# Down product of an expert ahead of the next expert's gate and up products, and early loads of ScalarE's function tables, in a two-layer mixer with 32 experts

## What is computed

```python
hdn = jax.nn.silu(xe @ w_gate[e]) * (xe @ w_up[e])     # 1024 -> 512
y_e = hdn @ w_down[e]                                  # 512 -> 1024
x   = x + gt2 * sum_of_two(gate * y_e)                 # after both layers: final RMSNorm
```

## Time and profile before

| | us |
|---|---|
| median of 3 runs (1959.91 to 1963.07) | 1959.96 |
| the profiled execution, its own time | 1950.96 |
| span of the profiled execution | 1949.1 |
| TensorE busy (matmul) | 1636.3 (84%) |
| VectorE busy | 622.2 (32%) |
| ScalarE busy | 447.4 (23%) |
| GpSimd busy | 209.1 (11%) |
| data moved by DMA | 527.50 MB |

### The profile page before, as it was taken

One profiled execution on the slowest core, in us unless ns is written; L12 is line 12 of the kernel. 1 busy time (PEld: TensorE's weight loads), 2 busy tenths in 40 slices (PEclk: granted clock), 3 DMA queues, 4 the chain that ended last, 5 costly groups with the idle time before them and its releaser, 6 DMA issues. The chain is left out here.

```text
span 1949.1 us, 22716 instructions
## 1 busy us (share of the span) xinstructions
PE 1636.3 (84%) x7580; PEld 809.3 (42%) x7580; DVE 622.2 (32%) x1333; ACT 447.4 (23%) x1003; POOL 209.1 (11%) x215
## 2 busy tenths in 40 slices
PE   4999987898878998888869999879689788888883
PEld 2455544454333333333335555454434333333331
DVE  1256365233222122222153825631421212221214
ACT  2110645311111111111121026551121111111112
POOL 2000022011111011111020002011110101110110
PEclk7999978998989999999979998889799989998987
DMA  9422434137999999999972324420499999999994
GB/s 340 166 87 96 164 112 143 44 138 282 405 403 401 377 400 408 402 415 412 388 255 69 126 75 161 149 87 22 144 364 379 402 413 405 404 411 395 396 398 186
DMA packets 119092, 527.50 MB, mean 271 GB/s; under 512 B 17008, under 2 KB 23248, under 8 KB 69872
## 3 DMA queue, kind: packets, MB, share of 16 engines
q1 hardware_dynamic: 101520, 493.66, 65.1%
q0 software_dynamic: 13104, 24.51, 4.0%
q10 hardware_dynamic: 4400, 8.46, 1.1%
HBM read 521.06 MB, written 23.86 MB: 280 GB/s over the span
## 5 line engine op out<-in xcount | busy, mean ns | idle before, releaser
L1182 PE MATMUL ps<-ring,arena 128*64 128x512 f32 x2928 | 701.2, 638 | 157.5 <-DMA ring<-in_w_exp_up 130.2
L1182 PEld LDWEIGHTS ps<-ring,arena 128*64 128x64 f32 x2928 | 252.1, 146 | 563.0 <-issue 532.4
L889 PE MATMUL ps<-ring,hT 128*128 128x512 f32 (+1 forms) x1024 | 373.6, 523 | 6.6 <-ACT tmp L1358 4.9
L889 PEld LDWEIGHTS ps<-ring,hT 128*128 128x128 f32 x1024 | 196.5, 195 | 166.5 <-issue 148.4
L622 DVE TENSOR_TENSOR arena<-ps,arena 64x512 f32<-64x512 f32 (+1 forms) x64 | 44.4, 693 | 662.7 <-ACT arena L1455 581.2
L1455 ACT ACTIVATE arena<-ps 128x512 f32<-128x512 f32 x64 | 38.2, 598 | 621.8 <-PE ps L1182 576.0
L1447 ACT ACTIVATE arena<-ps,modc 128x128 f32<-128x128 f32 x256 | 96.5, 457 | 264.6 <-PE ps L1167 264.5
L854 POOL DMA_INDIRECT yexp_d<-arena,masks x64 | 59.3, 927 | 902.6 <-DVE arena L632 902.6
L1589 DVE SCALAR_TENSOR_TENSOR probsT<-z,convw,probsT 128x512 f32<-128x512 f32 x120 | 90.0, 751 | 3.9
L630 DVE TENSOR_TENSOR arena<-ps,gate 64x512 f32<-64x512 f32 (+1 forms) x64 | 43.7, 683 | 145.6 <-PE ps L1182 131.1
L611 DVE TENSOR_SCALAR arena<-ps,modc 128x128 f32<-128x128 f32 x256 | 87.5, 405 | 7.0 <-PE ps L1167 3.6
(11 more groups left out here) (198 smaller groups left out, 1285.3 us busy)
## 6 DMA issues: line engine op xcount, KB each, us to landing
ring<-in_w_exp_gate SPq DMA_DIRECT2D x128, 1024.0 KB, 15.7
ring<-in_w_exp_up SPq DMA_DIRECT2D x128, 1024.0 KB, 19.0
ring<-in_w_exp_down SPq DMA_DIRECT2D x128, 1024.0 KB, 12.5
ring<-in_w_ada SPq DMA_DIRECT2D x24, 2048.0 KB, 8.8
ring<-in_w_in SPq DMA_DIRECT2D x8, 2048.0 KB, 20.4
ring<-in_w_out SPq DMA_DIRECT2D x4, 2048.0 KB, 7.8
ring<-in_w_in SPq DMA_DIRECT2D x6, 1024.0 KB, 10.5
xn_d<-arena ACTq DMA_DIRECT2D x8, 512.0 KB, 4.8
```

The lines of the kernel that those rows point to most:

```text
L889: last = pe.matmul(out, lhs(k), rhs(k), start=(k == 0), stop=(k == n - 1))
L1182: last = [pe.matmul(outs[c][HALF * c:HALF * c + HALF, :], lhs(k)[:, 0:HALF], rhs(c, k), start=(k == 0), stop=(k == n - 1), tile_position=( ...
```

## The change

TensorE runs down(e) straight after turn_hidden(e), ahead of gate_up(e+1); VectorE runs expert_rows(e) ahead of expert_hidden(e+1). ScalarE's, GpSimd's and SyncE's orders in the expert stage stay. On ScalarE, three activations of one column into a new tile `spare` are added in each layer: a square root after the issues of the row loads in `combine`, a square root before the loop that follows the attention, and a silu after the router's exponentials.

```diff
@@ tiles @@
+        spare = sb("spare", [P, 1])
@@ experts_dve @@
             expert_tokens(1, 1)
+            expert_rows(0, 0, 0)
             expert_hidden(1, 0, 1)
-            expert_rows(0, 0, 0)
             expert_tokens(2, 0)
+            expert_rows(1, 0, 1)
             expert_hidden(2, 1, 0)
-            expert_rows(1, 0, 1)
             expert_tokens(3, 1)
             with dve.Fori(1, HE - 1) as it:
+                expert_rows(2 * it, it, 0)
                 expert_hidden(2 * it + 1, it, 1)
-                expert_rows(2 * it, it, 0)
                 expert_tokens(2 * it + 2, 0)
+                expert_rows(2 * it + 1, it, 1)
                 expert_hidden(2 * it + 2, it + 1, 0)
-                expert_rows(2 * it + 1, it, 1)
                 expert_tokens(2 * it + 3, 1)
+            expert_rows(NE - 2, HE - 1, 0)
             expert_hidden(NE - 1, HE - 1, 1)
-            expert_rows(NE - 2, HE - 1, 0)
             expert_rows(NE - 1, HE - 1, 1)
@@ tensor @@
                     turn_hidden(2 * it, 0)
+                    down(2 * it, it, 0)
                     gate_up(2 * it + 1, it, 1)
-                    down(2 * it, it, 0)
                     turn_tokens(2 * it + 2, it + 1, 0)
                     turn_hidden(2 * it + 1, 1)
+                    down(2 * it + 1, it, 1)
                     gate_up(2 * it + 2, it + 1, 0)
-                    down(2 * it + 1, it, 1)
                     turn_tokens(2 * it + 3, it + 1, 1)
                 turn_hidden(NE - 2, 0)
+                down(NE - 2, HE - 1, 0)
                 gate_up(NE - 1, HE - 1, 1)
-                down(NE - 2, HE - 1, 0)
                 turn_hidden(NE - 1, 1)
                 down(NE - 1, HE - 1, 1)
@@ scalar, combine, after the row loads are issued @@
+                act.activation(spare[:, :], C["eps"], ACT.Sqrt)
@@ scalar, after the router's exponentials @@
+                act.activation(spare[:, :], C["eps"], ACT.Silu)
```

## The result

The changed kernel has a median of 1933.78 us (4 runs, 1932.45 to 1942.38) beside 1959.93 us before: ratio 0.9883, 95% interval 0.9859 to 0.9908. Two later comparisons with more runs gave 0.9898 (0.9879 to 0.9917) and 0.9895 (0.9872 to 0.9918), so some 20 us of 1957. The forecast of 1945 us had the sign and most of the mechanism. It stands 11 us above this first median, and its gain of 15 us is 5 short of the 20 that the later ratios give. The profiled execution has a span of 1932.5 us against 1949.1.

What follows compares the result with a forecast made beforehand. The prediction took the DMA weight stream, 16.2 us an expert, to bound the expert stages. Starts 7.5, wide experts 3.0 and ends 3.7 give 14.2, rounded to 15 us off the 1959.96 us median: 1945 us, range 1930 to 1956.

Steps and rivals of the forecast that it cites:

- What bounds the stage: Expert stages: the DMA engines' weight stream sets the pace, 16.2 us an expert at 404 GB/s; TensorE has spare time.
- The rule: Expert stages: the end moves only by idle DMA time between loads and TensorE's work after the last up weights land.
- Part 1: TensorE's own cycle per expert in the new order: 13.85 us at full clock, under the stream's 16.2, so no steady gain.
- Part 2: Start of each expert stage: idle DMA time goes because down(0) frees its slot earlier; 7.5 us for both layers.
- Part 3: Behind experts with more than 64 tokens: most idle DMA time goes as loads are released earlier; 3.0 us, bounds 0 and 4.2.
- Part 4: End of each expert stage: down(30) runs before the last landing, so down(31) starts 1.84 us earlier, 3.7 us in all.
- Part 5: ScalarE's function table loads, moved to idle time or earlier: 0 us, upper bound 2.6 us.
- The sum: Whole kernel: starts, wide experts and ends give 14.2 us, taken as 15 with some tenths for small ragged slices.
- TensorE as the bound: Expert stages: pauses around the hidden turn lower TensorE's clock, cycle 17.25 us, kernel slower at 1997 us; chance 8%.
- The third rival: More is won: wide-expert gain whole, tables on the path, stream above 404 GB/s; 1935 us or less; chance 13%.

Runs made afterwards that it cites:

- light pair: Kernel before and changed kernel, each weight load from the third expert on moving a quarter of its bytes: 1814.65 and 1851.20 us.
- light_after: Changed kernel with each weight load from the third expert on moving a quarter of its bytes: 1851.20 us, beside 1814.65 in the old order.
- start_only: Kernel before with the new order for experts 0 and 1 of each stage only: ratio to before 0.9944.
- the middle alone: Kernel before with the new order for experts 2 to 30 only, old order at experts 0, 1 and the last: ratio to before 0.9987.
- end_only: Kernel before with the new order for the last expert of each stage only: ratio to before 1.0002.
- before_again: Kernel before, unchanged, profiled a second time: ratio 0.9992.
- tables_only: Kernel before with only the early function table loads on ScalarE added, order unchanged: ratio to before 0.9998.

## Why the prediction was right, and where it was short

- **What bounds the stage** was right: the light pair shows from the other side that the stream was the cover, since without it the change loses 37 us. The rule that the end moves only through idle DMA time and the end of the stage holds in layer 0, where experts 20 to 30 are spaced at 15.9 and 16.0 us. In layer 1 it left something out: the stream itself ran 1.5% faster, 4 to 5 us.
- **Part 1** was right to 0.1 us: a cycle of 13.85 us, measured 13.8 to 13.9 at the start of the stages and 13.9 in light_after. Two small slips: the pause before the hidden turn was put at 0.5 us, while its own terms, 1.53 less 1.16, give 0.37 (measured 0.45 to 0.55), and the pauses alone can lower the clock now and then, as light_after shows.
- **Part 2**, the starts, predicted 7.5 us: start_only has 9.1 to silu(30), 9.5 to gate_up(31), 10.1 to down(31) and 11 by its ratio. Right in mechanism, a fifth or more too small; the bytes missing in the two holes give 8.6.
- **Part 3** is the step that failed, in its size: predicted 3.0 us, bounds 0 and 4.2. To the start of gate_up(31) the middle alone measures 6.7 us and 14.9 - 9.5 = 5.4 on top of the starts. I read the loss from the busy share, and took 1.2 us off for a lag that did no harm; the bytes moved in the same windows would have given 6.6. The windows behind the wide experts are full now, but no run had the wide experts alone, and in layer 1 the faster stream is in the same sum.
- **Part 4**, the ends, predicted 1.84 us each: in the changed kernel the down product starts 2.2 us earlier after gate_up(31). The premise, that down(30) then lies before the last landing, holds in the changed kernel and not in end_only. The difference of 0.4 is that down(31) no longer waits for VectorE to empty its banks of down(30)'s rows (the pause before it is 0.69 us, where the earlier trace rows have 0.98), and that the turn starts 1.44 us behind the silu instead of my 1.53. What of it reaches the end was only seen in end_only: there 0.9 us of layer 0's 2.2 were left where the next layer's projections run.
- **Part 5**, the tables, predicted 0: ratio 0.9998.
- **The sum.** The terms give 14.2 us; the 0.8 that make it 15 had no row. Starts and wide experts were put at 10.5 us and measure 14.9 (to gate_up(31)); the ends were put at 3.7 and measure 20.0 - 14.9 = 5.1. To the last silu of layer 1 the first profile of before was 2.4 and 3.2 us quicker than before_again and tables_only, and so 16.6 us between the two first profiles agreed with my 15 by chance.
- **The rivals.** TensorE as the bound was wrong for this kernel, and the clock went the other way: the waits for weights are now 61.0 / 36 = 1.7 us instead of 3.0, the mean clock is 0.942 instead of 0.920. The Trainium skill ("TensorE: Matmul & The Clock Gate", section "HAM oscillation") sees the danger in waits for data between short pieces of compute; the trace agrees that the long waits mattered, and the reordering cut them into shorter ones. The third rival came true in part. Its sign, a rate above 404 GB/s, is there: 411 in the window at 1640 us, and 405 instead of 401 over 1700 to 1860 us. Part 3 came whole, and the first median, 1933.78 us, lies in its "1935 or less". The tables gave nothing, and in layer 0 the experts kept their pace.

## What to carry to other kernels

In a stage that streams weights through a ring, use the slots in the order in which they are loaded: a use out of order holds back every load behind it, and most of the price shows where the queue runs dry, at the start and behind slow pieces. Measure such holes by the bytes that are missing, not by the busy share. Read a partial change by the whole stage, to its last product: the middle alone had 8.8 us at expert 30 and 2.6 at the end. A reordering that puts pauses on the compute engine is free only as long as the stream covers them; how much cover there is can be measured by loading a quarter of the bytes.

## What the runs showed of the hardware that was not expected

The DMA share falls slowly at the end of a stream, as if the 16 engines did not finish together. DMA slices of the changed kernel, 1860 to 1900 us, 1 us each:

```profile
DMA  9999999999999999999997654544333441110000
GB/s 451 410 401 426 422 447 369 336 418 434 410 410 442 434 410 410 410 442 406 438 410 295 254 229 205 213 180 180 139 164 131 160 152 74 78 61 16 0 0 16
```

No load of the ring is issued after about 1873 us, and the share falls from 9 tenths at 1881 step by step to 1 tenth at 1895, while gate_up(31) still waits for its weights until 1889.5. Before the change the fall took about 5 us. I read it so: a deeper queue lets the quicker engines run ahead by as much as the ring allows, and a load has landed only when the slowest engine has brought its share. No row of these traces names a single engine, so this is a reading and not shown. What it costs can be seen from the bytes. Queue q1 from the start of the span to 956.84 us before and to 948.72 us after, which is 486.3 and 476.0 us from layer 0's first silu:

```profile
q1 hardware_dynamic: 54169, 251.45, 67.5%
q1 hardware_dynamic: 54210, 251.43, 67.7%
```

The bytes are 10.3 us earlier, but gate_up(31), which waits for the last up weights, starts only 7.1 us earlier (487.9 and 480.7). In layer 1 q1 has moved 487.5 MB by 1901.4 and 1882.4 us, 11.1 us earlier from the first silu, and gate_up(31) starts 6.4 us earlier. So nearly 8 us of what the fuller queue won in bytes did not arrive at TensorE. Which engines lag, and why, was not tried and stays open.
